# Expert activations turned by VectorE in 32x32 blocks, with gate and up strips taken in runs of 32 columns

## The chip, the cores and the metric

One core of one Trainium2 chip runs the kernel. The metric is the device time of one execution, in microseconds. One execution was also recorded by the hardware profiler, and all rows in this document come from such recordings.

## What is computed

One layer of a hybrid diffusion backbone over 640 tokens of 1024 values (128 context tokens, 512 latent tokens): a modulated norm, a token mixer (mLSTM heads and a Hyena long convolution), and then a mixture of experts. Everything is float32. The change touches the experts alone:

```python
def hier_moe(x, p):
    ...
    # coarse top-1 of 4 groups, then top-2 of 4 experts in it
    gates = jnp.sum(jax.nn.one_hot(expert_ids, N_EXPERTS, dtype=jnp.float32) * w_sel[..., None], axis=1)
    hg = jnp.einsum('td,edf->tef', xt, p['w_gate'])
    hu = jnp.einsum('td,edf->tef', xt, p['w_up'])
    act = jax.nn.silu(hg) * hu * gates[:, :, None].astype(x.dtype)
    return jnp.einsum('tef,efd->td', act, p['w_down']).reshape(bsz, seq_len, d)
```

There are 16 experts, each with a gate matrix and an up matrix of 1024 x 512 and a down matrix of 512 x 1024 (2 MiB each, 6 MiB per expert). Each token uses two experts.

## The kernel before

The program writes the instruction stream of each engine by hand and orders the engines by semaphores. The expert stage is the last large one. The tokens that chose an expert are packed into **groups** of 32 rows; each expert has at least two groups, and the profiled inputs give 48 groups in all. TensorE runs the groups in the order of the experts, in one hardware loop per expert (`pe.Fori`), and handles a group in three steps.

- **`gate_and_up(i, e)`** (matmul at L1919). The stationary operand is one 128 x 32 block of the group's input, `xg`, already turned. The array is split into four column strips of 32 (`LANES`, q = 0 to 3), and strip q computes hidden columns q*128 to q*128+127 of gate and of up at once, 256 columns in one moving operand. Over 8 blocks k of the contraction that makes 32 matmuls. The profile shows a float32 matmul as two records, so 64 records. The result stands in PSUM bank 2: partition 32q+r holds row r of the group, the first 128 columns are gate, the next 128 are up.
- **`down(i, e)`** (L1930), 16 matmuls or 32 records of 256 columns, again in four strips. The stationary operand is a 128 x 32 slice of `aT`, the turned activation, and the moving operand the down matrix. It runs one group behind: TensorE does `gate_and_up(i)`, `down(i - 1)`, `turn_act(i)`.
- **`turn_act(i)`** (L1938), one TensorE transpose of the whole 128 x 128 activation `uact` into PSUM bank 4.

The other engines work around this order. VectorE (loop at L1413 to L1424) turns the input rows of the next group in 32 x 32 blocks (`turn_rows`, L1400), multiplies silu(gate) by up into `uact` (L1420, signal `act_ready`), copies half of the down result out (`y_out`, L1407), and copies the turned activation from PSUM to SBUF as `aT` (L1424, signal `aT_d`). ScalarE computes silu (L868), copies the other half of the down result (L849) and issues the store of 128 KB to DRAM (L855). GpSimd issues an indirect load (L533) that gathers the rows of a later group, 32 rows of 4 KB.

The **weights** go through three sets of buffers. The SyncE queue issues the gate and up loads of expert e+3 once `gu_done` shows that the last gate-and-up of expert e has finished, and its down load once `down_done` shows the same of the last `down` (L436). At the start of an expert TensorE waits until its gate and up loads have landed (L1954), and before its first `down` for the down load. After the last group comes `y_out`, a gather of all expert outputs and the final norm, which use neither loads nor TensorE.

The waits that order a group on VectorE and TensorE:

```python
dve.wait_ge(S["at_t"], i)          # ahead of the multiply into uact
dve.wait_ge(S["at_t"], i + 1)      # ahead of the copy to aT
dve.wait_ge(S["down_done"], i)
pe.wait_ge(S["act_ready"], i)      # ahead of gate_and_up(i): bank 2 has been read
pe.wait_ge(S["aT_d"], i + 1)       # ahead of down(i)
```

Of the kernel before, what the change touches and what calls it, by code (L numbers as in the profile page):

```python
# [13 lines left out]
P = 128  # L14
D = 1024
KD = D // P
# [13 lines left out]
NG, NE, EPG = 4, 16, 4  # L30
FF = 512
LANE = 32
UNITS = 2 * H
ROWS = 36
LANE = 32
LANES = P // LANE
# [65 lines left out]
def emit(nc, a, stack):  # L102
# [7 lines left out]
    ps = stack.enter_context(nc.psum_tensor("banks", [P, 8, 512], F32))  # L110
# [67 lines left out]
    ident = small(128)  # L178
# [80 lines left out]
    set_at = [(0, F0 + 2 * SLOT, SLOT), (2 * SLOT, F0 + SLOT, F0), (W2 + 5120, W2 + 5120 + SLOT, W0)]  # L259
# [3 lines left out]
    xg = area(E0 + 512, KD, LANE)  # L263
    gact = area(E0 + 768, P)
    uact = area(E0 + 896, P)
    aT = area(E0 + 1024, P)
# [4 lines left out]
    def rt(*shape):  # L271
# [32 lines left out]
        e_ready w_ready s_done p_ready kw_ready inter_done inter_read intra_done num_ready upd_done st_ready  # L304
        h_ready hsq hss hrs yml_ready yt_done yt_read wo_done wo_sq wo_ss wo_rs x2_sq x2_rs h2_ready h2t_done h2t_read
        lg_done rt_v rt_exp pos_done idx_done tiles_ready route_ready
        idx_taken xg_ready gu_done silu_ready act_ready at_t aT_d down_done y_a y_d
        comb_s comb_v comb_rs fin_ready act_chain dve_chain pool_chain""".split()
    S = {n: sem(n) for n in names}
    ld_max = [sem(f"ld_max{i}") for i in range(2)]  # L310
# [42 lines left out]
    def start_at_one(eng, *signals):  # L353
        for name in signals:
            eng.sem_inc(S[name], 1)
# [535 lines left out]
    def _(dve):  # L891
# [32 lines left out]
        for o in range(ORD):  # L924
            for w in range(10):
                t, s, n = w // 2, w % 2, 20 * o + w
# [18 lines left out]
            for g in (1, 3, 5, 7):  # L945
# [12 lines left out]
                first, second = spec_h[:, o, part, blk + 1, :], ps[:, 1 + n % 4, :]  # L958
# [26 lines left out]
        for n in range(1, 10, 2):  # L985
# [6 lines left out]
            else:  # L992
                k = n - 2
# [4 lines left out]
        for n in range(12):  # L998
            part, blk = ((2, 0, 1)[n // 4], n % 4)
            dve.wait_ge(S["conv_a"], n + 1)  # L1000
            u = part1t[:, blk, :] if part == 1 else ubuf[:, n % 2, :]
# [190 lines left out]
        for i in range(NSTEP):  # L1192
            d, t = steps[i]
# [219 lines left out]
        with dve.Fori(0, pairs) as pair:  # L1413
            for n in range(2):
                i = 2 * pair + 1 + n
                dve.wait_ge(S["gu_done"], i + 1)
                turn_rows(1 - n, 16 * pair + 16 + 16 * n)
                dve.wait_ge(S["silu_ready"], i + 1)
                dve.wait_ge(S["at_t"], i)
                dve.tensor_tensor(uact, ps[:, 2, P:2 * P], gact, ALU.mult).then_inc(S["act_ready"], 1)  # L1420
                y_out(i - 1, n, 16 * pair + 16)
                dve.wait_ge(S["at_t"], i + 1)
                dve.wait_ge(S["down_done"], i)
                dve.tensor_copy(aT, ps[:, 4, 0:P]).then_inc(S["aT_d"], 1)  # L1424


        pairs = dve.value_load(tiles_i[0:1, 16:17], min_val=MINGROUPS // 2, max_val=GROUPS // 2)
# [10 lines left out]
        for t in range(NT):  # L1438
# [3 lines left out]
            s = st1[:, 60 + t:61 + t]  # L1442
# [4 lines left out]
    def _(pe):  # L1447
        M = pe.matmul
# [72 lines left out]
        for o in range(ORD):  # L1521
            for w in range(10):
                t, s, n = w // 2, w % 2, 20 * o + w
# [11 lines left out]
            for g in range(10):  # L1535
# [4 lines left out]
                if g >= 8:  # L1540
                    mm = M(ps[:, b, :], dft_c[:, 9 - g, :], ab[:, 9 - g, 0, :], start=True, stop=True)
                else:
                    f, odd = (g % 4) // 2 * P, (1 - g % 2) if part == 0 else g % 2
                    for i in range(2):
                        tb = 2 * odd + i
                        mm = M(ps[:, b, :], dft_l[:, tb, part, f:f + P], ab[:, part, 1 + tb, :], start=i == 0, stop=i == 1)  # L1546
                mm.then_inc(S["filt_done"], 1)
                if g == 0:
                    pe.wait_ge(S["lanes_read"], 2 * o + 2)
                    for i, rows in enumerate((P, 2 * LANE)):  # L1550
                        mm = M(ps[0:1, 5 + i, :], lane_pick[0:rows, :], lane_sums[i], start=True, stop=True)
# [4 lines left out]
                if g == 7:  # L1556
                    pe.wait_ge(S["norm_sqrt"], 2 * o + 2)
                    for i in range(2):
                        for blk in range(NB):
                            c = i * NB + blk  # L1560
                            mm = M(ps[:, 6, c:c + 1], norm_rows[i][:, blk * P:(blk + 1) * P], ones[0:1, 0:1],
                                   start=True, stop=True)
# [6 lines left out]
        for n in range(10):  # L1569
# [3 lines left out]
            for q in range(4):  # L1573
                t, k = (0, 4 * n + q) if n < 2 else (1 + q, n - 2)
                mm = pe.transpose(ps[:, b, q * P:(q + 1) * P], x_raw[:, t, k * P:(k + 1) * P], ident)
# [76 lines left out]
        for t in range(NT):  # L1652
            b = inverse_bank(t)
            if t < LT:
                for fb in range(2):
                    pe.wait_ge(S["mul_done"], fb + 1)
                    for part in range(2):
                        mm = M(ps[:, b, :], idft_l[:, fb, part, t * P:(t + 1) * P], spec_x[:, part, 2 * fb + t // 2, :],  # L1658
                               start=fb == 0 and part == 0, stop=fb == 1 and part == 1)
            else:  # L1660
                pe.wait_ge(S["mul_done"], 3)
                M(ps[:, b, :], dft_c[:, 2, :], spec_xc[:, 0, :], start=True, stop=False)
                mm = M(ps[:, b, :], dft_c[:, 3, :], spec_xc[:, 1, :], start=False, stop=True)
# [5 lines left out]
        for n in range(5):  # L1669
            b = inverse_bank(NT + n)  # L1670
            if n < NB:
                for r in range(2):
                    half = slice(r * LAT // 2, (r + 1) * LAT // 2)
                    for fb in range(2):
                        pe.wait_ge(S["mul_done"], 4 + fb)
                        for part in range(2):
                            mm = M(ps[:, b, half], spec_x[:, part, 2 * fb + r, n * P:(n + 1) * P],  # L1677
                                   idft_l[:, fb, part, half], start=fb == 0 and part == 0, stop=fb == 1 and part == 1)
            else:
                pe.wait_ge(S["mul_done"], 6)  # L1680
                for c in range(NB):
                    M(ps[:, b, c * P:(c + 1) * P], spec_xc[:, 0, c * P:(c + 1) * P], dft_c[:, 2, :], start=True, stop=False)
                    mm = M(ps[:, b, c * P:(c + 1) * P], spec_xc[:, 1, c * P:(c + 1) * P], dft_c[:, 3, :],
                           start=False, stop=True)
# [4 lines left out]
        for b, lo, hi in ((7, CTX, TOK), (0, 0, CTX)):  # L1689
            for step in range(KD // LANES):  # L1690
                for lane in range(LANES):
                    k = lane * (KD // LANES) + step
                    mm = M(ps[lane * LANE:(lane + 1) * LANE, b, 0:hi - lo], wgate[:, k, :], hT[:, k, lo:hi],
                           start=step == 0, stop=step == KD // LANES - 1)
# [3 lines left out]
        for t in range(NT):  # L1698
            if t >= 4:
                pe.wait_ge(S["qk_read"], 2 * NB + t - 3)  # L1700
            for h in range(H):
                mm = pe.transpose(ps[:, 1 + t % 4, h * P:(h + 1) * P], kT[:, h, t * P:(t + 1) * P], ident)
# [5 lines left out]
        for i in range(2):  # L1708
            M(ps[0:ROWS, 5 + i, :], gate_pick[:, i, :], gate_parts[:, CTX:TOK], start=True, stop=True)
            mm = M(ps[0:ROWS, 0, i * P:(i + 1) * P], gate_pick[:, i, :], gate_parts[:, 0:CTX], start=True, stop=True)  # L1710
# [26 lines left out]
        for n, (t0, t1) in enumerate(((0, 3), (3, 5))):  # L1737
            for t in range(t0, t1):
                for q in range(4):
                    c = ((t - t0) * 4 + q) * ROWS  # L1740
                    mm = pe.transpose(ps[:, 5 + n, c:c + ROWS], g_q[:, q, t * P:(t + 1) * P], ident[0:ROWS, 0:ROWS])
# [4 lines left out]
        for u in range(UNITS):  # L1746
            mm = M(ps[:, 7, u * NT:(u + 1) * NT], sel[:, u, :], dec, start=True, stop=True)
# [14 lines left out]
        for i in range(NSTEP):  # L1762
            d, t = steps[i]
# [124 lines left out]
        first = [1] + first_groups(1, 6)  # L1888

        def row_numbers(hot, lo, ready):  # L1890

            pe.wait_ge(S["rt_v"], ready)
            for n in range(2 * NT):
# [13 lines left out]
        first += first_groups(8, NE + 1)  # L1907

        gate_up = [mem[:, g:g + 2 * (u - g)].rearrange("p (s w) -> p s w", s=2)[:, :, 0:SLOT]
                   .rearrange("p s (k f) -> p s k f", k=KD) for g, u, d in set_at]  # L1910
        downs = [area(d, FF // P, D) for g, u, d in set_at]

        def gate_and_up(i, e):

            pe.wait_ge(S["xg_ready"], i + 2)
            pe.wait_ge(S["act_ready"], i)
            for k in range(KD):
                for q in range(LANES):
                    mm = M(ps[q * LANE:(q + 1) * LANE, 2, 0:2 * P].rearrange("p (g f) -> p g f", g=2), xg[:, k, :],  # L1919
                           gate_up[e % 3][:, :, k, q * P:(q + 1) * P], start=k == 0, stop=k == KD - 1)  # L1920
            mm.then_inc(S["gu_done"], 1)

        def down(i, e):
# [7 lines left out]
                           downs[e % 3][:, q, l * 256:(l + 1) * 256], start=q == 0, stop=q == FF // P - 1)  # L1931
            mm.then_inc(S["down_done"], 1)

        def turn_act(i):

            pe.wait_ge(S["act_ready"], i + 1)
            pe.wait_ge(S["aT_d"], i)
            pe.transpose(ps[:, 4, 0:P], uact, ident).then_inc(S["at_t"], 1)  # L1938

        start_at_one(pe, "gu_done", "down_done", "at_t")  # L1940
        for full in w_full[0][0:2]:
            pe.wait_ge(full, 16)
        gate_and_up(1, 0)
        turn_act(1)
        for e in range(NE):
            loads = 16 * (e // 3 + 1)
            with pe.Fori(first[e] + 1, first[e + 1]) as i:
                gate_and_up(i, e)
                pe.wait_ge(w_full[e % 3][2], loads)
                down(i - 1, e)  # L1950
                turn_act(i)
            if e + 1 < NE:
                for full in w_full[(e + 1) % 3][0:2]:
                    pe.wait_ge(full, 16 * ((e + 1) // 3 + 1))  # L1954
                gate_and_up(first[e + 1], e + 1)
            down(first[e + 1] - 1, e)
            if e + 1 < NE:
                turn_act(first[e + 1])


# [24 lines left out]
```

## Time and profile before

| | us |
|---|---|
| median of 3 runs | 918.48 |
| lowest, highest | 917.35, 919.62 |
| the profiled execution, its own time | 917.74 |
| its span, first to last instruction | 915.9 |
| TensorE busy | 827.9 (90% of the span) |
| VectorE, ScalarE, GpSimd busy | 409.7, 269.1, 107.0 |
| mean granted TensorE clock | 0.967 of full |
| data moved by DMA | 191.41 MB |

A row names the engine (PE is TensorE's matmuls, PEld its weight loads, DVE is VectorE, ACT is ScalarE, POOL is GpSimd, SPq the queue of SyncE), the line of the code, the operation, and the output and input tile. All SBUF tiles are parts of `arena`, and all PSUM tiles parts of `banks`, so that the line tells which tile it is. Matmuls overlap in the array: their starts show the pace, their durations do not add up.

### The profile page before, as it was taken

The page shows a single profiled execution, that of the slowest core. Times are in us where ns is not written, and L with a number is a line of the kernel's source. Part 1 is how long each engine was busy: PE and PEld are TensorE (multiplying, and loading weights), DVE is VectorE, ACT ScalarE, POOL GpSimd, SP SyncE. Part 2 cuts the span into 40 slices and gives each one's busy share as a digit, 9 for nine tenths or more (in the row PEclk, how much of TensorE's full clock was granted, in tenths as well). Part 3 has the DMA queues.
Part 4 walks back from the last instruction along what each step waited for, and adds up shares of the span by engine and source line. Part 5 has one row for each costly group of instructions (what it writes and reads, how often), then busy time and mean ns, then how long its engine had stood idle before and what let it go on. Part 6 is the DMA issues. An engine that isn't in the chain of part 4 may idle for free.

```text
span 915.9 us, 17241 instructions
## 1 busy us (share of the span) xinstructions
PE 827.9 (90%) x6857; PEld 449.2 (49%) x6857; DVE 409.7 (45%) x799; ACT 269.1 (29%) x541; POOL 107.0 (12%) x210
## 2 busy tenths in 40 slices
PE   5898999999999999997998999789999999999900
PEld 1242555555355457554664455455555555555500
DVE  5645721121492491555444774833333333333335
ACT  1676411210200100327232332123333333333332
POOL 4000000000001000001001000022222222222140
PEclk9999999999999999999999999799999999999965
DMA  8958303140705302033009203999999999995162
GB/s 258 414 229 321 127 1 115 69 184 1 275 1 171 109 1 92 24 116 115 1 1 340 119 24 132 418 352 412 417 422 416 418 420 415 419 421 195 41 243 113
DMA packets 40202, 191.41 MB, mean 209 GB/s; under 512 B 4416, under 2 KB 4712, under 8 KB 32529
## 3 DMA queue, kind: packets, MB, share of 16 engines
q1 hardware_dynamic: 28426, 152.50, 41.7%
q0 software_dynamic: 9168, 31.61, 10.0%
q10 hardware_dynamic: 2552, 6.50, 2.0%
q8 instruction: 43, 0.70, 0.3%
q14 instruction: 13, 0.11, 0.0%
HBM read 174.14 MB, written 16.44 MB: 208 GB/s over the span
## 4 chain that ended last, share of the span: by engine, by line
PE 81%; DVE 6%; DMA 5%; ACT 4%; issue 1%; SPq 1%; POOL 0%; DVEq 0%; ACTq 0%; POOLq 0%
PE banks L1919 19%; PE banks L1584 15%; PE banks L1930 9%; PE banks L1814 4%; PE banks L1585 4%; PE banks L1824 4%; PE banks L1546 3%; PE banks L1625 3%; PE banks L1720 3%; DMA arena<-in_w_ada 3%; PE banks L1729 2%; PE banks L1478 2%; ACT arena L755 2%; PE banks L1677 2%; PE banks L1658 1%
## 5 line engine op out<-in xcount | busy, mean ns | idle before, releaser
L1919 PE MATMUL banks<-arena 128*32 128x256 f32 x3072 | 175.7, 381 | 1.5 <-DVE arena L1400 1.5
L1584 PE MATMUL banks<-arena 128*128 128x512 f32 x320 | 164.2, 595 | 2.6 <-ACT arena L708 1.6
L1919 PEld LDWEIGHTS banks<-arena 128*32 128x32 f32 x3072 | 95.7, 110 | 64.9 <-issue 2.3
L1585 PEld LDWEIGHTS banks<-arena 128*128 128x128 f32 x320 | 60.8, 190 | 76.5 <-issue 76.5
L1400 DVE STREAM_TRANSPOSE arena<-arena 128x256 f32<-128x256 f32 x49 | 32.2, 656 | 137.3 <-PE banks L1919 134.4
L1930 PE MATMUL banks<-arena 128*32 128x256 f32 x1536 | 91.7, 379 | 1.0 <-DVE arena L1424 1.0
L1930 PEld LDWEIGHTS banks<-arena 128*32 128x32 f32 x1536 | 50.0, 110 | 33.8 <-DVE arena L1424 1.2
L1585 PE MATMUL banks<-arena 128*128 128x128 f32 x320 | 61.5, 274 | 0.0
L1407 DVE COPY arena<-banks 32x256 f32<-32x256 f32 x98 | 41.4, 422 | 40.6 <-PE banks L1930 39.9
L849 ACT ACTIVATE arena<-banks 32x256 f32<-32x256 f32 x98 | 36.6, 374 | 71.5 <-PE banks L1930 70.9
L1584 PEld LDWEIGHTS banks<-arena 128*128 128x128 f32 x320 | 48.5, 192 | 6.1 <-issue 4.9
L1007 DVE SCALAR_TENSOR_TENSOR arena<-banks,arena 128x504 f32<-128x504 f32 x12 | 8.9, 743 | 89.4 <-ACT arena L685 89.4
L533 POOL DMA_INDIRECT arena<-expert_input,arena x47 | 46.2, 984 | 12.5 <-issue 12.5
L868 ACT ACTIVATE arena<-banks 128x128 f32<-128x128 f32 x48 | 13.3, 277 | 99.0 <-PE banks L1919 99.0
L1729 PE MATMUL banks<-arena 128*128 128x512 f32 x80 | 37.7, 616 | 5.1 <-ACT arena L747 3.3
L865 ACT ACT_TABLE_LOAD x24 | 30.8, 1283 | 28.4 <-DVE arena L1407 22.1
L1814 PE MATMUL banks<-arena 128*128 128x512 f32 x80 | 36.8, 617 | 2.5 <-ACT arena L747 2.5
L1824 PE MATMUL banks<-arena 128*128 128x512 f32 x80 | 35.5, 597 | 1.7 <-DVE arena L1229 1.7
L684 ACT ACTIVATE arena<-banks,arena 128x512 f32<-128x512 f32 x12 | 8.2, 687 | 94.5 <-PE banks L1585 94.5
L1720 PE MATMUL banks<-arena 128*128 128x512 f32 x80 | 34.9, 595 | 0.0
L1546 PE MATMUL banks<-arena 128*128 128x512 f32 x64 | 28.8, 600 | 2.3 <-DVE arena L921 2.3
L530 POOL COPY arena<-arena 128x1 int32 x47 | 8.5, 181 | 182.0 <-DVE arena L1400 182.0
(380 smaller groups left out, 1025.2 us busy)
## 6 DMA issues: line engine op xcount, KB each, us to landing
arena<-in_w_gate SPq DMA_DIRECT2D x16, 2048.0 KB, 21.2
arena<-in_w_up SPq DMA_DIRECT2D x16, 2048.0 KB, 26.4
arena<-in_w_down SPq DMA_DIRECT2D x16, 2048.0 KB, 25.8
arena<-in_w_ada SPq DMA_DIRECT2D x12, 2048.0 KB, 13.7
arena<-in_w_in SPq DMA_DIRECT2D x7, 2048.0 KB, 7.9
expert_output<-arena ACTq DMA_DIRECT2D x49, 128.0 KB, 6.3
expert_output<-arena POOLq DMA_DIRECT2D x1, 4096.0 KB, 20.9
arena<-in_w_out SPq DMA_DIRECT2D x2, 2048.0 KB, 7.7
```

What stands on the lines that cost most here:

```text
L533: pool.indirect_dma_start(xr[n], None, h2_quarters, bass.IndirectOffsetOnAxis(ap=idx_now[n], axis=0))\
L849: ins = act.activation(ysb[n][:, l * 256:(l + 1) * 256], ps[l * LANE:(l + 1) * LANE, 5, 0:256], ACT.Copy)
L1407: ins = dve.tensor_copy(ysb[n][:, l * 256:(l + 1) * 256], ps[l * LANE:(l + 1) * LANE, 5, 0:256])
L1546: mm = M(ps[:, b, :], dft_l[:, tb, part, f:f + P], ab[:, part, 1 + tb, :], start=i == 0, stop=i == 1)
L1584: M(ps[:, b, :], lhs, hT[:, k, CTX:TOK], start=k == 0, stop=k == KD - 1)
L1585: mm = M(ps[:, b + 1, 0:CTX], lhs, hT[:, k, 0:CTX], start=k == 0, stop=k == KD - 1)
L1720: mm = M(ps[:, 1 + n % 4, :], hT[:, k, n * P:(n + 1) * P], w[:, k, :], start=k == 0, stop=k == KD - 1)
L1729: mm = M(ps[:, 1, :], hT[:, k, t * P:(t + 1) * P], w[:, k, :], start=k == 0, stop=k == KD - 1)
L1814: M(ps[:, 1 + 2 * (j % 2) + c, :], part1t[:, k, t * P:(t + 1) * P], w[:, NB + k, :], start=k == 0, stop=False)
L1824: mm = M(ps[:, 1 + 2 * (j % 2) + c, :], ymlT[:, k, t * P:(t + 1) * P], w[:, k, :], start=False, stop=k == NB - 1)
L1919: mm = M(ps[q * LANE:(q + 1) * LANE, 2, 0:2 * P].rearrange("p (g f) -> p g f", g=2), xg[:, k, :], gate_up[e % 3][:, :, k, q * P:(q + 1) * ...
L1930: mm = M(ps[l * LANE:(l + 1) * LANE, 5, 0:256], aT[:, q * LANE:(q + 1) * LANE], downs[e % 3][:, q, l * 256:(l + 1) * 256], start=q == 0, s ...
```

## The change

`turn_act` and its signal `at_t` go. VectorE now turns `uact` itself, from SBUF to SBUF, in place of its copy out of PSUM. Its transpose turns each 32 x 32 block where it stands, so block a of strip q, which holds four times 32 hidden columns, lands in partitions 32q to 32q+31 and columns 32a to 32a+31 of `aT`. For `aT[:, 32a:32a+32]` to be the 128 rows a*128 to a*128+127 that `down` wants, strip q must compute the columns a*128 + 32q + j (a = 0 to 3, j = 0 to 31). So the moving operand of `gate_and_up` takes four runs of 32 columns, 128 apart, in gate and again in up: 8 runs of 32 instead of 2 runs of 128. The down matrix and the loads stay as they are.

```diff
@@ VectorE, expert loop @@
                 dve.wait_ge(S["silu_ready"], i + 1)
-                dve.wait_ge(S["at_t"], i)
+                dve.wait_ge(S["aT_d"], i)
                 dve.tensor_tensor(uact, ps[:, 2, P:2 * P], gact, ALU.mult).then_inc(S["act_ready"], 1)
                 y_out(i - 1, n, 16 * pair + 16)
-                dve.wait_ge(S["at_t"], i + 1)
+                dve.wait_ge(S["act_ready"], i + 1)
                 dve.wait_ge(S["down_done"], i)
-                dve.tensor_copy(aT, ps[:, 4, 0:P]).then_inc(S["aT_d"], 1)
+                dve.transpose(aT, uact).then_inc(S["aT_d"], 1)
@@ TensorE @@
         gate_up = [mem[:, g:g + 2 * (u - g)].rearrange("p (s w) -> p s w", s=2)[:, :, 0:SLOT]
-                   .rearrange("p s (k f) -> p s k f", k=KD) for g, u, d in set_at]
+                   .rearrange("p s (k a q j) -> p s k q a j", k=KD, q=LANES, j=LANE) for g, u, d in set_at]
...
-                    mm = M(ps[q * LANE:(q + 1) * LANE, 2, 0:2 * P].rearrange("p (g f) -> p g f", g=2), xg[:, k, :],
-                           gate_up[e % 3][:, :, k, q * P:(q + 1) * P], start=k == 0, stop=k == KD - 1)
+                    mm = M(ps[q * LANE:(q + 1) * LANE, 2, 0:2 * P].rearrange("p (g a j) -> p g a j", g=2, j=LANE), xg[:, k, :],
+                           gate_up[e % 3][:, :, k, q, :, :], start=k == 0, stop=k == KD - 1)
...
-        def turn_act(i):
-
-            pe.wait_ge(S["act_ready"], i + 1)
-            pe.wait_ge(S["aT_d"], i)
-            pe.transpose(ps[:, 4, 0:P], uact, ident).then_inc(S["at_t"], 1)
...
         gate_and_up(1, 0)
-        turn_act(1)
         for e in range(NE):
             loads = 16 * (e // 3 + 1)
             with pe.Fori(first[e] + 1, first[e + 1]) as i:
                 gate_and_up(i, e)
                 pe.wait_ge(w_full[e % 3][2], loads)
                 down(i - 1, e)
-                turn_act(i)
...
             down(first[e + 1] - 1, e)
-            if e + 1 < NE:
-                turn_act(first[e + 1])
```

In TensorE's stream, the first expert's loop and the way into the second, before. L1947 is the loop, L1915 the wait for the next expert's gate and up loads:

```order
L1919 MATMUL banks<-arena 32x256 [waits act_ready,xg_ready]
L1919 MATMUL banks<-arena 32x256 x31
L1930 MATMUL banks<-arena 32x256 [waits y_a,y_d,aT_d,w_full02]
L1930 MATMUL banks<-arena 32x256 x15
L1936 REGISTER_ALU
L1938 MATMUL banks<-arena 128x128 [waits aT_d,act_ready]
L1947 REGISTER_ALU
L1947 COMPARE_AND_BRANCH
L1915 REGISTER_ALU [waits w_full11,w_full10]
L1919 MATMUL banks<-arena 32x256 [waits act_ready,xg_ready]
```

The same place with the change, where L1940 is the loop:

```order
L1919 MATMUL banks<-arena 32x256 [waits act_ready,xg_ready]
L1919 MATMUL banks<-arena 32x256 x31
L1930 MATMUL banks<-arena 32x256 [waits y_a,y_d,aT_d,w_full02]
L1930 MATMUL banks<-arena 32x256 x15
L1940 REGISTER_ALU
L1940 COMPARE_AND_BRANCH
L1915 REGISTER_ALU [waits w_full11,w_full10]
L1919 MATMUL banks<-arena 32x256 [waits act_ready,xg_ready]
```

The one matmul between `down` and the next `gate_and_up` is gone, with its two waits; all else keeps its place.

On VectorE, one group of the loop, as a piece of the difference:

```order
 L1400 STREAM_TRANSPOSE arena<-arena 128x256 [waits gather1]
 L1419 REGISTER_ALU [waits silu_ready]
-L1420 TENSOR_TENSOR arena<-banks,arena 128x128 [waits at_t]
+L1420 TENSOR_TENSOR arena<-banks,arena 128x128 [waits aT_d]
 L1407 COPY arena<-banks 32x256 [waits y_stored0,down_done]
 L1407 COPY arena<-banks 32x256
-L1424 COPY arena<-banks 128x128 [waits down_done,at_t]
+L1424 STREAM_TRANSPOSE arena<-arena 128x128 [waits down_done,act_ready]
```

The copy becomes a block transpose at the same place, and both waits on `at_t` become waits on VectorE's own earlier signals.

## Rows read from the trace of the kernel before

**Rows 1.** Page, part 4: the chain that ended last, shares of the span by line
```profile
PE banks L1919 19%; PE banks L1584 15%; PE banks L1930 9%; PE banks L1814 4%; PE banks L1585 4%; PE banks L1824 4%; PE banks L1546 3%; PE banks L1625 3%; PE banks L1720 3%; DMA arena<-in_w_ada 3%; PE banks L1729 2%; PE banks L1478 2%; ACT arena L755 2%; PE banks L1677 2%; PE banks L1658 1%
```
**Rows 2.** Timeline from 640 us: start, us, engine, line, op, out<-in, count, [idle before <-releaser]
```profile
640.24 3.66 PE L1919 MATMUL banks<-arena 128*32 128x256 f32 x64
...
643.72 1.91 PE L1930 MATMUL banks<-arena 128*32 128x256 f32 x32
...
644.06 0.66 DVE L1400 STREAM_TRANSPOSE arena<-arena 128x256 f32<-128x256 f32 x1 [2.76 <-PE banks L1919]
644.64 0.25 DVE L1420 TENSOR_TENSOR arena<-banks,arena 128x128 f32<-128x128 f32 x1
...
645.56 0.33 PE L1938 MATMUL banks<-arena 128*128 128x128 f32 x1
...
645.70 0.86 DVE L1407 COPY arena<-banks 32x256 f32<-32x256 f32 x2 [0.81 <-PE banks L1930]
645.82 3.18 PEld L1919 LDWEIGHTS banks<-arena 128*32 128x32 f32 x64
```
**Rows 3.** Timeline of PE, cut inside a group
```profile
642.86 1.05 PE L1919 MATMUL banks<-arena 128*32 128x256 f32 x16
...
644.80 0.83 PE L1930 MATMUL banks<-arena 128*32 128x256 f32 x12
```
**Rows 4.** The chain of waits in time: start, us, what
```profile
645.63 0.26 PE banks L1938
645.89 3.59 PE banks L1919 x64
649.48 1.73 PE banks L1930 x32
```
**Rows 5.** DMA, 20 us stretches: busy PE, PEld, DVE, ACT, POOL, clock, DMA share, GB/s
```profile
760.00:780.00 20.00, 20.00 (x352) 11.25 (x348) 7.15 (x18) 5.72 (x16) 4.93 (x12) 1.00 1.01 416
...
840.00:860.00 20.00, 20.00 (x352) 11.21 (x346) 7.18 (x19) 5.91 (x14) 5.43 (x12) 1.00 0.17 51
```
**Rows 6.** Up load issues of experts 8, 12 (SyncE), then each one's gate-and-up landing
```profile
683.39 0.44 SPq L436 DMA_DIRECT2D arena<-in_w_up  x1
DMA to landing us min/median/max: 22.7/25.3/27.9
...
750.33 0.43 SPq L436 DMA_DIRECT2D arena<-in_w_up  x1
DMA to landing us min/median/max: 23.4/25.9/28.5
```
**Rows 7.** Timeline of PE: starts of group 2, expert 8, expert 12, last group
```profile
606.77 3.66 PE L1919 MATMUL banks<-arena 128*32 128x256 f32 x64
...
718.34 1.93 PE L1919 MATMUL banks<-arena 128*32 128x256 f32 x32
...
785.28 3.66 PE L1919 MATMUL banks<-arena 128*32 128x256 f32 x64
...
863.39 3.66 PE L1919 MATMUL banks<-arena 128*32 128x256 f32 x64
```
**Rows 8.** Timeline of PE and DVE after the last gate-and-up
```profile
868.84 0.86 DVE L1407 COPY arena<-banks 32x256 f32<-32x256 f32 x2 [0.81 <-PE banks L1930]
869.73 0.29 DVE L1424 COPY arena<-banks 128x128 f32<-128x128 f32 x1
...
870.08 1.93 PE L1930 MATMUL banks<-arena 128*32 128x256 f32 x32 [1.04 <-DVE arena L1424]
```
**Rows 9.** Timeline of PE: small matmuls of 80 columns (L1875) and 64 (L1899)
```profile
585.72 0.45 PE L1875 MATMUL banks<-arena 128*128 128x80 f32 x2 [2.18 <-DVE arena L1330]
...
596.35 0.43 PE L1899 MATMUL banks<-arena 128*128 128x64 f32 x2 [0.43 <-DVE arena L1365]
```
**Rows 10.** PE after a long idle time, and the stretch around it (columns as rows 5)
```profile
432.12 5.26 PE L1729 MATMUL banks<-arena 128*128 128x512 f32 x8 [3.33 <-ACT arena L747]
...
430.00:436.00 6.00, 3.88 (x6) 1.77 (x7) 0.98 (x2) 1.95 (x3) 1.88 (x3) 0.72 0.39 88
```

More of the change, by code:

```diff
@@ L306, in emit @@
         lg_done rt_v rt_exp pos_done idx_done tiles_ready route_ready
-        idx_taken xg_ready gu_done silu_ready act_ready at_t aT_d down_done y_a y_d
+        idx_taken xg_ready gu_done silu_ready act_ready aT_d down_done y_a y_d
         comb_s comb_v comb_rs fin_ready act_chain dve_chain pool_chain""".split()
@@ L1932, in down @@
             mm.then_inc(S["down_done"], 1)
-        def turn_act(i):
-            pe.wait_ge(S["act_ready"], i + 1)
-            pe.wait_ge(S["aT_d"], i)
-            pe.transpose(ps[:, 4, 0:P], uact, ident).then_inc(S["at_t"], 1)
-        start_at_one(pe, "gu_done", "down_done", "at_t")
+        start_at_one(pe, "gu_done", "down_done")
         for full in w_full[0][0:2]:
```

## The prediction

> **What bounds the kernel now.** I read the page's chain first. The expert stage's two matmul lines, L1919 and L1930, make 28% of the span [rows 1], the largest share of any stage. The timeline then shows one group: gate-and-up from 640.24, down from 643.72, the turn at 645.56, the next gate-and-up at 645.82 [rows 2]. One group takes 5.58 us from gate-and-up to gate-and-up. TensorE has no idle time in it. VectorE and ScalarE wait for TensorE: VectorE sits idle 2.76 us before it turns the input rows [rows 2]. So in this stage each microsecond that TensorE saves counts, as long as nothing else is late.
>
> The DMA windows show what may be late. From 760 to 780 us the DMA share is 1.01, at 416 GB/s, and only at 840 to 860 is it down to 0.17 [rows 5]. The 16 DMA engines are full while experts are loaded. They are not on the chain before because the loads run ahead. How far ahead, the issue rows tell: the up load of expert 8 is issued at 683.39 and lands 27.9 us later, at 711.3, for a start of that expert at 718.34; that of expert 12 is issued at 750.33, lands at 778.8, and the expert starts at 785.28 [rows 6, 7]. The lead is 7.0 and 6.5 us. A faster TensorE can use that much and no more, as long as the transfers don't get faster too, and with full DMA engines an earlier issue doesn't make them so.
>
> **The change, part by part.**
>
> *The turn goes from TensorE.* What does it hold up? Within a phase four records, one per strip, start together. 16 records take 0.86 us (642.86 to 643.72) across the border from gate-and-up to down [rows 3, 2], so a four takes 0.216 us and that border costs nothing. The last 12 records of down start from 644.80 on [rows 3], so the last four starts at 645.23. The turn starts 0.33 us after it instead of 0.216, and the next gate-and-up 0.26 us after the turn [rows 2]. Without the turn a group is 24 fours x 0.216 = 5.18 us, against 5.58: **0.40 us per group**. The lower bound is the 0.26 us that the chain puts on the turn, beside 3.59 and 1.73 for the matmuls [rows 4]. I take 0.40, since the row of the unbroken border is the same kind of border that the change leaves behind. The Trainium skill (TensorEngine Tiling (Array Packing), Key Properties) says that changing the tiling mode drains TensorE; by this rule the change takes out two switches, into the full array and back, and the saving is more than the transpose itself, 0.40 and not 0.26. The late start of the turn agrees.
>
> *Strips with runs of 32.* The same 64 records, 256 columns each, now read in 8 runs instead of 2. No row shows this shape. The nearest: gate-and-up with 2 runs and down with 1 run keep the same 0.216 us. Farther off, two records of 80 columns whose input is 16 runs of 5 take 0.45 us, and two of 64 columns in one run take 0.43 us [rows 9]; the 16 extra columns alone explain the 0.02. I take zero, with a bound of 0.02 us per group for a gain or a loss by noise in these rows; a large price is a rival below. The output columns in PSUM are as contiguous as before.
>
> *The waits on TensorE.* The next gate-and-up still waits for `act_ready`, which the turn used to wait for. The multiply ends at 644.89, the last four of down starts at 645.23 [rows 2, 3]: 0.3 us to spare, and with the turn gone TensorE asks for it 0.6 us after it came (645.45). So the wait doesn't take the place of the turn. ScalarE's silu ends before the multiply and has the same cover.
>
> *VectorE: copy out, block transpose in.* The copy takes 0.29 us [rows 8]. The transpose of 128 x 256 takes 0.66 us [rows 2], so one of 128 x 128 costs between 0.33 (half of it) and 0.66; I take 0.37, nearer to the half, since its columns are halved. It follows the two copies of 0.86 us [rows 2]. `down` wants `aT` only after a whole gate-and-up of 3.5 us, and 0.86 + 0.37 lies well inside. It costs nothing there. The one place without cover is the last group, where the last down waits for it [rows 8]: +0.1 us. If the transpose took all the 0.66 us it would be +0.4.
>
> *The first group.* Group 2's gate-and-up starts at 606.77 [rows 7], right behind the turn of group 1, which no `down` covers. Without the turn it starts once the multiply is done. That saves between nothing and the turn's 0.26 us [rows 4]; I take 0.2, as only the multiply's wait stays.
>
> *Stores and gathers* keep their number (128 KB out and 128 KB in per group), but come closer together while the loads run.
>
> **The sum.** By TensorE alone: from group 2 (606.77) to the last group (863.39) there are 46 pitches [rows 7]; 0.2 + 46 x 0.40 - 0.1 = 18.5 us. But the loads set a floor. Expert 8 starts 20 pitches after group 2 ((718.34 - 606.77)/5.58): TensorE would be there 8.2 us earlier, and its lead is 7.0, so it waits about one us. Expert 12 starts 32 pitches after group 2; TensorE would be there 13.0 us earlier, and its load lands only 6.5 us before the old start. What moves that landing: -0.2, as the first refill is issued earlier; +0.6, as TensorE is one group ahead and so one more group's 0.26 MB passed at 416 GB/s [rows 5]. So it lands at 779.2, and TensorE starts about 0.4 us after a landing (an estimate between nothing and 0.67, the time from the multiply's end to the turn's start [rows 2], where the turn also waits for the array). That gives 779.6, a gain of 5.7 us. The experts from 13 on are safe: from 785.28 to 863.39 there are 14 pitches, 14 x 0.40 = 5.6 us more, and DMA falls to a share of 0.17 in this time [rows 5]. Then -0.1 at the last down. **5.7 + 5.6 - 0.1 = 11.2 us.** The tail is unchanged. 917.74 - 11.2 = 906.5 for the profiled execution; the median of the runs lay 0.7 above it, so **907.3**.
>
> With 0.26 us per group in place of 0.40, expert 12 still waits for its load, and the gain is 5.7 + 3.6 - 0.1 = 9.2 (909.3). That the landing moves by 2 us either way gives 905.3 to 909.3. Where an earlier expert's wait is long, nothing adds up: it only uses the same lead.
>
> **The rivals.**
>
> 1. *The loads keep up.* If earlier issues made earlier landings, the gain is 18.5 us and the time 900.0. For it: up loads take 28 us from issue to landing, so the queue is deep. Against it: a DMA share of 1.01 [rows 5], which leaves nothing to speed up. Chance 0.07.
>
> 2. *The waits for loads cost clock as well.* Before expert 12 TensorE would stand about 3 us or more, longer if the last down ends early. In this trace an idle time of 3.33 us stands before a stretch whose granted clock is 0.72 on average [rows 10], that is part of it at 1.2 GHz instead of 2.4. 0.28 x 6 us of that stretch is 1.7 us of lost work. After expert 12 that is not won back: 909.0. The Trainium skill (TensorE: Matmul & The Clock Gate, Why this matters for your kernels) warns against idle gaps between bursts of matmuls for this reason; by it the time would be this one. Against it: the stall I work out is a little shorter than the one in the row, since TensorE loses about 1 us at experts 8 to 10 already and arrives later. Chance 0.15.
>
> 3. *The runs of 32 read slower: slower than before.* Place: the 16 fours of gate-and-up in all 48 groups. If the start of a run cost time, there are 6 more per record. It decides from the point where it eats the 18.5 us of TensorE's gain: 18.5/48 = 0.39 us per group, 24 ns on each four of 216. For a result over 0.3% slower it takes 0.45 us per group, 28 ns per four, and the time is 921.3; at half the read rate it is +3.45 x 48 - 18.5 = +147 us, 1065. For it: no row has this shape. Against it: one or two runs make no difference, nor do 16 runs of 5 beyond 0.02 us [rows 9]. Chance 0.04.
>
> 4. *Something on the short loop is late*, such as the gathered rows of the next group, whose transfer shares the full DMA engines and now has two pitches of 5.18 instead of 5.58 to land. VectorE's 2.76 us idle before its turn of the input rows is put down to TensorE [rows 2], so the rows were there. If they came late by some 0.1 us in most groups up to expert 12, the load floor would hide it; it would cost only behind it, where DMA goes idle. Price up to 2 us: 909.3. Chance 0.07.
>
> **How the numbers follow.** The forecast, a gain bounded by the load of expert 12 or its neighbour, has 0.67. The range has to hold landings that move by 2 us, the smaller saving of 0.26, the clock rival, and part of the way to rival 1: 903.5 to 911.0. Outside are rival 1, rival 3 and the ends. About 0.3% (2.8 us) is what a measurement of this kernel can tell from no change. Everything but rival 3, and a small rest in which a partial read price meets the load floor, is faster by more than that: faster 0.93, same 0.03, slower 0.04.
>
> **What would show it.** Right: inside an expert the pitch is 5.18 us with no L1938; idle time of TensorE before L1919 at the starts of experts 8 to 12 that ends on a landing of `in_w_up`; the DMA share stays 1.0 to about 837 us; the block transpose at L1424 takes 0.33 to 0.45 us; the last gate-and-up starts some 11 us before 863.39. Wrong: a four of gate-and-up longer than 0.216 us (rival 3), no idle time at expert starts (rival 1), a granted clock under 1.0 behind a wait (rival 2), VectorE's turn of the rows waiting for a gather (rival 4).

## The result and the profile after

The changed kernel takes **911.76 us** (median of 4 runs, 909.31 to 913.53), the kernel before 918.85 (4 runs): ratio 0.9916, 95% interval 0.9891 to 0.9940, 7 to 8 us faster. Run again beside three of the experiments it took 911.11 against 920.48, ratio 0.9903 (0.9885 to 0.9922). The forecast of 907.3 had the direction right; the time lies 0.8 us above its range. The profiled execution took 909.31, the fastest of the four, so it is set against 917.74.

One group of the loop, from the changed kernel's timeline (columns as in rows 2; L1424 is now the block transpose):

```profile
641.45 1.94 PE L1930 MATMUL banks<-arena 128*32 128x256 f32 x32
...
641.81 0.66 DVE L1400 STREAM_TRANSPOSE arena<-arena 128x256 f32<-128x256 f32 x1 [2.47 <-PE banks L1919]
...
642.50 0.29 DVE L1420 TENSOR_TENSOR arena<-banks,arena 128x128 f32<-128x128 f32 x1
...
643.18 3.66 PE L1919 MATMUL banks<-arena 128*32 128x256 f32 x64
...
644.23 0.29 DVE L1424 STREAM_TRANSPOSE arena<-arena 128x128 f32<-128x128 f32 x1
...
646.63 1.94 PE L1930 MATMUL banks<-arena 128*32 128x256 f32 x32
```

From one down to the next it is 646.63 - 641.45 = 5.18 us, where rows 2 had 5.58 for a group. The next gate-and-up starts 1.73 us after down, with nothing between. It takes 3.45 us from its start to the next down with its 8 runs, where rows 2 have 3.48 with 2 runs.

TensorE's starts that answer to rows 7 and 8, from the same timeline:

```profile
602.14 3.66 PE L1919 MATMUL banks<-arena 128*32 128x256 f32 x64
606.92 3.66 PE L1919 MATMUL banks<-arena 128*32 128x256 f32 x64 [1.12 <-DVE arena L1420]
...
713.01 3.66 PE L1919 MATMUL banks<-arena 128*32 128x256 f32 x64 [1.92 <-DMA arena<-in_w_up]
...
729.37 3.66 PE L1919 MATMUL banks<-arena 128*32 128x256 f32 x64 [0.61 <-DMA arena<-in_w_up]
...
746.55 3.66 PE L1919 MATMUL banks<-arena 128*32 128x256 f32 x64 [1.43 <-DMA arena<-in_w_up]
...
781.74 5.15 PE L1919 MATMUL banks<-arena 128*32 128x256 f32 x64 [3.90 <-DMA arena<-in_w_up]
786.70 1.92 PE L1930 MATMUL banks<-arena 128*32 128x256 f32 x32
...
862.33 1.93 PE L1930 MATMUL banks<-arena 128*32 128x256 f32 x32 [1.19 <-DVE arena L1424]
```

TensorE waits for the up load at experts 8, 9, 10 and 12, 7.9 us in all. The prediction had about 1 us for experts 8 to 10; they took 4.0, but each of these waits only uses up the same lead. The page's chain now has `DMA arena<-in_w_up` at 8%. The first gate-and-up of expert 12 takes 4.96 us instead of 3.45. The windows say why (columns as in rows 5):

```profile
612.00:775.00 163.00, 158.88 (x2936) 114.81 (x2931) 61.40 (x153) 54.33 (x123) 41.72 (x92) 1.00 1.01 417
...
780.00:790.00 10.00, 8.27 (x128) 4.99 (x132) 2.01 (x5) 1.02 (x3) 1.36 (x3) 0.83 1.03 429
```

The granted clock was full up to there, with the DMA engines full; behind the idle time of 3.90 us it is 0.83 over 10 us, as much as 3.4 us at 1.2 GHz instead of 2.4. That costs 4.96 - 3.45 = 1.5 us.

The start of the stage moves by some microseconds from execution to execution (601.78 before, 602.14 and 599.96 in two profiles of the changed kernel). So I compare the **stage length**, from TensorE's first gate-and-up to its last down: 870.08 - 601.78 = 268.30 before, 862.33 - 602.14 = 260.19 after, 260.54 in the second profile. The stage gives 8.1 of the profiled 8.4 us. The two pairs of medians, 7.1 and 9.4 us apart, lie on both sides of it.

### The profile page after: what moved, and what is told of

It is laid out like the page before. It is cut to its first block, busy times and chain, and to the rows that moved or that the text cites. A ratio compares the mean times of both kernels' runs of the same rounds, so it can differ in the third digit from the quotient of the medians.

```text
span 907.5 us, 17049 instructions
## 1 busy us (share of the span) xinstructions
PE 813.7 (90%) x6809; PEld 470.7 (52%) x6809; DVE 411.5 (45%) x799; ACT 269.0 (30%) x541; POOL 107.6 (12%) x210
## 4 chain that ended last, share of the span: by engine, by line
PE 74%; DMA 12%; DVE 6%; ACT 4%; issue 1%; SPq 1%; POOL 0%; DVEq 0%; ACTq 0%
PE banks L1584 15%; PE banks L1919 14%; DMA arena<-in_w_up 8%; PE banks L1930 6%; PE banks L1585 4%; PE banks L1824 4%; PE banks L1814 4%; PE banks L1546 3%; PE banks L1625 3%; PE banks L1720 3%; DMA arena<-in_w_ada 3%; PE banks L1729 2%; PE banks L1478 2%; ACT arena L755 2%; PE banks L1677 2%; PE banks L1658 2%
## 5 line engine op out<-in xcount | busy, mean ns | idle before, releaser
L1919 PE MATMUL banks<-arena 128*32 128x256 f32 x3072 | 177.1, 382 | 9.1 <-DMA arena<-in_w_up 7.9
L1919 PEld LDWEIGHTS banks<-arena 128*32 128x32 f32 x3072 | 115.4, 111 | 62.7 <-issue 12.5
L1930 PEld LDWEIGHTS banks<-arena 128*32 128x32 f32 x1536 | 57.6, 110 | 26.6 <-DVE arena L1424 1.7
```

Source lines behind the costliest of these rows:

```text
L1930: mm = M(ps[l * LANE:(l + 1) * LANE, 5, 0:256], aT[:, q * LANE:(q + 1) * LANE], downs[e % 3][:, q, l * 256:(l + 1) * 256], start=q == 0, s ...
```

## The experiments

All are timed against the kernel before on the same chip; the rows come from several chips, so compare ratios and stages rather than medians. Stage length as above; the start of expert 12 is counted from the start of the stage.

| kernel | median us | ratio to before, 95% | stage us | expert 12 at |
|---|---|---|---|---|
| before | 918.85 | | 268.30 | 183.50 |
| changed | 911.76 | 0.9916 (0.9891-0.9940) | 260.19 | 179.60 |
| changed, again | 911.11 | 0.9903 (0.9885-0.9922) | 260.54 | 179.75 |
| runs of 32 alone | 920.33 | 1.0004 (0.9987-1.0022) | 268.34 | |
| VectorE's turn alone | 911.77 | 0.9912 (0.9880-0.9943) | 260.49 | 179.71 |
| before, light loads | 920.08 | 0.9999 (0.9981-1.0017) | 268.29 | |
| changed, light loads | 900.71 | 0.9793 (0.9765-0.9821) | 249.64 | |
| light, runs of 128 | 900.61 | 0.9795 (0.9773-0.9817) | 249.63 | |
| light, two turns | 900.00 | 0.9778 (0.9761-0.9794) | 249.94 | |
| two down loads smaller | 909.17 | 0.9875 (0.9854-0.9897) | 257.67 | 176.89 |
| filler at expert 12 | 909.33 | 0.9884 (0.9864-0.9903) | 258.69 | 179.60 |
| halves | 910.84 | 0.9904 (0.9881-0.9928) | 259.72 | |
| halves, early refill | 909.41 | 0.9881 (0.9861-0.9901) | 257.07 | |
| halves, early, filler | 908.79 | 0.9871 (0.9852-0.9889) | 257.63 | |
| no gathers | one run | | 249.64 | |
| more SyncE code | one run | | 263.26 | 182.48 |

**1. Each half of the change alone.** Runs of 32 with TensorE's turn kept:

```diff
# the kernel before, plus
+                   .rearrange("p s (k a q j) -> p s k q a j", k=KD, q=LANES, j=LANE) for g, u, d in set_at]
+                           gate_up[e % 3][:, :, k, q, :, :], start=k == 0, stop=k == KD - 1)
```

> The kernel before with only the runs of 32 in gate-and-up; TensorE keeps its turn, so down multiplies activations with rows of the down matrix that belong to other columns. Theory (the gain is capped by the weight loads, and the runs of 32 are free): same as before within 0.3%, pitch of a group 5.58 us, a four of gate-and-up 0.216 us. Rival (runs of 32 cost reading time, and this took part of the gain): slower by 1 to 4 us, pitch above 5.6 us.

The stage is 268.34 us, as before. A group of this kernel in the timeline:

```profile
644.30 3.66 PE L1919 MATMUL banks<-arena 128*32 128x256 f32 x64
647.78 1.91 PE L1930 MATMUL banks<-arena 128*32 128x256 f32 x32
649.62 0.33 PE L1938 MATMUL banks<-arena 128*128 128x128 f32 x1
649.88 3.66 PE L1919 MATMUL banks<-arena 128*32 128x256 f32 x64
```

5.58 us, and 3.48 from gate-and-up to down as in rows 2. The other half, VectorE's turn with the strips' old columns (the `gate_up` lines of the kernel before in the changed kernel):

> The changed kernel with the strips' old columns (2 runs of 128): only the turn moves to VectorE, and down multiplies activations with rows of the down matrix that belong to other columns. Theory: as the changed kernel, 909 to 913.5 us, pitch 5.18 us, waits for up loads at expert 8 to 12. Rival (runs of 32 cost): faster than the changed kernel by 1 to 4 us.

911.77 us, stage 260.49: the whole gain is in the turn, for in the stage the two full kernels lie 7.8 to 8.1 us apart and this one 7.8. The runs of 32 are only needed so that `down` meets the right rows, and they cost nothing.

**2. The load floor taken away.** In both kernels experts 3 to 15 load a quarter of the down matrix, so that the loads run well ahead of TensorE. (The rest of each down buffer holds an older expert's rows; TensorE's work is the same.)

```diff
                 sp.wait_ge(S[done], used)
+                if done == "down_done":
+                    dst, src = dst[:, 0:1, :], src[:, 0:1, :]
                 sp.dma_start(dst, src).then_inc(full, 16)
```

> The kernel before, where experts 3 to 15 load only the first quarter of their down matrix (1.5 MiB less of 6 per expert; the rest of the buffer holds an older expert's rows). Theory: TensorE never waited for loads before, so nothing changes: within 0.3% of before. Rival (full DMA engines also slow the pace of TensorE or the late tail): 1 to 5 us faster.

> The changed kernel with the same quarter of down loads from expert 3 on. Theory (load floor): no waits on up loads, no fall of the clock at expert 12, the whole 46 pitches x 0.40 us come out: 18 us under the light kernel before, near 900 us, and runs that scatter less. Rival (the floor is something else, such as gathers or a wait in the loop): stays at 905 to 912 us.

The kernel before doesn't change (268.29). The changed one falls to 900.71 us, and its stage to 249.64: 18.7 us shorter than before, where TensorE's side of the sum said 18.5. No wait for a load is left among TensorE's waits over the stage:

```profile
PE banks L1921 <- DVE arena L1402: 1.4, 1, 1.4
PE banks L1932 <- DVE arena L1426: 1.2, 1, 1.2
PE banks L1901 <- DVE arena L1367: 1.1, 1, 1.1
PE banks L1921 <- DVE arena L1422: 1.1, 1, 1.1
```

and its window shows DMA engines that are not full, with the clock at 1.00:

```profile
612.00:775.00 163.00, 163.00 (x3028) 118.81 (x3024) 63.54 (x159) 56.40 (x127) 43.65 (x96) 1.00 0.92 369
```

So of the 18.7 us that the missing turn is worth, 10.5 to 10.9 are lost again to the weight loads and to the clock that falls behind a wait for them.

**3. The same floor, moved by a known amount.** The down loads of experts 3 and 4 alone bring three of four quarters:

```diff
                 sp.wait_ge(S[done], used)
+                if done == "down_done" and e in (3, 4):
+                    dst, src = dst[:, 0:3, :], src[:, 0:3, :]
                 sp.dma_start(dst, src).then_inc(full, 16)
```

> The changed kernel where the down loads of experts 3 and 4 bring only three quarters (0.5 MB less each, 2.5 us less for the DMA engines at 416 GB/s; the last quarter holds an older expert's rows). Theory (until expert 12 the DMA engines set the pace): start of expert 12 comes 2.5 us earlier after the start of the stage, its wait stays near 3.8 us, time 2.5 us under the changed kernel. Rival (the waits come from single late loads): the wait at expert 12 and the time stay as they were within 1 us.

Expert 12 starts 176.89 us into the stage instead of 179.60 and 179.75: 2.7 to 2.9 us earlier. The stage is 2.5 to 2.9 us shorter. (The medians, 909.17 against 911.11 and 911.76, agree, but their intervals overlap.) The wait is still there:

```profile
779.89 5.35 PE L1921 MATMUL banks<-arena 128*32 128x256 f32 x64 [3.71 <-DMA arena<-in_w_up]
```

So up to expert 12 the DMA traffic sets the pace: 2.5 us of it taken away came out as 2.5 to 2.9 us. The rival, single late loads, falls.

**4. What hides on VectorE, and the runs without a floor.** On the light changed kernel:

```diff
+                dve.transpose(fold, uact)
                 dve.transpose(aT, uact).then_inc(S["aT_d"], 1)
```

> The light changed kernel (down loads quartered from expert 3 on), where VectorE turns the activation twice in every group, the first time into an unused tile. Theory (VectorE's turn is hidden, but for the last group): 0.3 us over the light changed kernel, 900 to 902 us. Rival (VectorE is near the bound once TensorE is faster): 0.29 us in each group, 14 us more.

> The light changed kernel with the strips' old columns (2 runs of 128), where no load floor can hide a price of the runs of 32. Theory: as the light changed kernel within 1 us, the same 3.45 us from the first record of gate-and-up to the first of down. Rival (runs of 32 cost): faster by over 1 us.

A second turn in all 48 groups adds 0.30 us to the stage. Of it 0.19 is at the last down, the only place without cover, whose wait grows from 1.19 to 1.38 us; 0.1 comes once, at an expert's start 41 us into the stage, and I don't know from what. In all other groups it is hidden. With runs of 128 the stage is 249.63, with runs of 32 249.64: no price of the runs can be seen, 0.01 us over 48 groups.

**5. The clock at expert 12.** The filler:

```diff
+            if e + 1 in FILL:              # FILL = {12: 4}
+                stay_busy(FILL[e + 1])
             if e + 1 < NE:
                 for full in w_full[(e + 1) % 3][0:2]:
```

> The changed kernel with four idle matmuls of 128x512 (3.4 us, result unused) that TensorE runs ahead of its wait for the loads of expert 12, where it stood 3.9 us. Theory (the wait also costs clock: 3.4 us at 1.2 GHz, 1.5 us of work): granted clock stays at its high level at expert 12, 0.5 to 1.5 us faster than the changed kernel, less than the full 1.5 if the landing comes before the filler ends. Rival (the clock's fall costs nothing that counts): same as the changed kernel, or slower by the filler's overhang.

```profile
777.37 3.70 PE L1872 MATMUL banks<-arena 128*128 128x512 f32 x8
781.35 3.66 PE L1920 MATMUL banks<-arena 128*32 128x256 f32 x64 [0.28 <-issue]
784.80 1.94 PE L1931 MATMUL banks<-arena 128*32 128x256 f32 x32
```

Expert 12 starts at the same 179.60, but its gate-and-up takes 3.45 us again, and the stage is 1.5 to 1.9 us shorter than the changed kernel's, where 0.5 to 1.5 was expected. The medians, 909.33 and 911.11, say the same, though their intervals overlap. The clock's fall costs 1.5 us or a little more, near the 1.7 worked out from rows 10.

**6. Taking time off the floor.** Gate and up loads in two halves each; then the first half refilled from the middle of the old expert's last gate-and-up (`gu_half`); then with a filler of three between the halves:

```diff
+            for h in range(2):
+                for i, src in enumerate(srcs[0:2]):
+                    k = slice(KD // 2 * h, KD // 2 * (h + 1))
+                    yield area(set_at[e % 3][i], KD, FF)[:, k, :], src[:, k, :], w_full[e % 3][h]
...
             for k in range(KD):
+                if k == KD // 2 and second is not None:
+                    pe.wait_ge(w_full[e % 3][1], second)
...
+                if k == KD // 2 - 1:
+                    mm.then_inc(S["gu_half"], 1)
```

> The changed kernel with each expert's gate and up loads cut in two along the contraction: first blocks 0 to 3 of both, then 4 to 7; the first gate-and-up of an expert starts on the first halves and waits for the second in its middle. Theory (waits on the landing of up loads cap the gain): expert 12 finishes its first gate-and-up up to 1.7 us earlier after the landing, and the long idle time is cut in two shorter ones, so the clock may stay high: 1.5 to 3 us faster than the changed kernel, 907.5 to 910. Rival (total DMA time alone sets the pace, whatever the order in an expert, or the smaller loads land later): same as the changed kernel within 1 us, or slower.

> As the kernel with halves, and the first halves of a set are refilled once TensorE is half through the old expert's last gate-and-up, 1.7 us earlier. In the trace the DMA engines stand idle for about 3 us between the first nine loads (607.5) and the first refill (610.5). Theory: all later landings come 1.7 us earlier, so 1 to 2 us faster than the halves alone, 906 to 908.5. Rival (the landings follow from something else than the start of the refills): same as the halves alone.

> Halves, early refill, and three idle matmuls of 128x512 (2.6 us) between the two halves of the first gate-and-up of expert 12. Theory (waits and the clock's fall add up): no fall of the clock at expert 12, half a gate-and-up less behind the landing, 1 to 2 us faster than the halves with early refill (909.4) or than the filler alone (909.3): 907.5 to 908.5. Rival (what is saved before expert 12 only makes its wait longer): 909 to 910, as these two.

The halves alone miss their 907.5 to 910: 910.84 us, not to be told from the changed kernel (the stage is 0.5 to 0.8 us shorter). TensorE ran the first half ahead of the landing, but then stood as long in its middle, and the clock fell all the same:

```profile
777.21 1.91 PE L1924 MATMUL banks<-arena 128*32 128x256 f32 x32
783.02 2.57 PE L1924 MATMUL banks<-arena 128*32 128x256 f32 x32 [3.90 <-DMA arena<-in_w_up]
```

With the early refill the stage is 257.07 us, 2.6 less than with the halves alone, where 1 to 2 was expected. The refill itself gave 1.0 of it: the second half of expert 12 starts 179.69 us into the stage instead of 180.65, not 1.7 earlier. The rest comes from the clock, which did not fall in this execution, although the wait was 3.79 us:

```profile
783.14 1.94 PE L1924 MATMUL banks<-arena 128*32 128x256 f32 x32 [3.79 <-DMA arena<-in_w_up]
```

So its median of 909.41 (906 to 908.5 expected) is no proof of what the refill is worth. All three together give **908.79 us**, the fastest by its median of those that do the whole computation, 1.3% under the kernel before; its interval still touches that of the changed kernel. I expected 907.5 to 908.5. The filler brought the stage nothing there (257.63): the clock had not fallen without it in that profile, and the load landed 0.6 us later.

**7. Why the landing was late.** The up load of expert 12 lands at 781.39 in the changed kernel, issued at 745.16 with 36.2 us to its landing:

```profile
745.16 0.56 SPq L436 DMA_DIRECT2D arena<-in_w_up  x1
...
DMA to landing us min/median/max: 31.4/33.8/36.2
```

That is 179.3 us into the stage, against 177.1 before. The trace has 16 steps of the load's semaphore as it lands, with the time of each. There are 16 DMA engines, and I read each step as one engine's piece of the load. Before and after, the first piece of expert 12's up load came 173.7 and 173.9 us into the stage, and the last 3.4 and 5.4 us behind the first. It is not one piece alone that moved: the first is 0.1 us later than before, the mean of the 16 is 0.8 later, the last but one 1.1 and the last 2.2. The repeat of the changed kernel has the same picture (5.6 us between first and last). Nor is so wide a spread new: the kernel before has 5.7 us at expert 13, where nobody waits for the load.

Two kernels ask what makes the last piece late. Without the gathers of the loop, so that experts compute on old rows:

```diff
-            pool.indirect_dma_start(xr[n], None, h2_quarters, bass.IndirectOffsetOnAxis(ap=idx_now[n], axis=0))\
-                .then_inc(gather[n], 16)
+            pool.dma_start(xr[n][0:1, :], h2_quarters[0:1, :]).then_inc(gather[n], 16)
```

> The changed kernel where the 47 gathers of 128 KB inside the loop become loads of one row of 1 KB, so experts compute on old rows. In the changed kernel the first of the 16 pieces of expert 12's up load lands 5.4 us before the last; in the kernel before it was 3.4 us. Theory A (the gathers load the 16 DMA engines unevenly): the spread falls under 2 us. Theory B (it is code fetches or the weight loads themselves): the spread stays at 3 us or more. Both: 33 x 0.13 MB less before expert 12, so its landing comes about 10 us earlier, no waits for loads, the stage as short as in the light kernel (249.6 us from its first matmul to the last down).

The spread stays at 4.5 us, so the gathers are not what mainly makes it. Their bytes, though, were part of the floor: expert 12's load lands 11.8 us earlier, there are no waits for loads, and the stage is 249.64 us. With more code on SyncE, after each expert's loads:

```diff
                 sp.dma_start(dst, src).then_inc(full, 16)
+            for _ in range(192):
+                sp.wait_ge(S["ld_setup"], 112)
```

> The changed kernel where SyncE passes 192 waits that are already met after each expert's loads, so that its code fetches (16 KB pieces of the instruction queues, 1.0 to 1.1 us each on a DMA engine) grow by about 13 between experts 3 and 15. Theory B1 (code fetches hold up single DMA engines, and so the last piece of a load): more than 24 fetches in the stage, and the spread of expert 12's up load grows from 5.4 by 1 us or more. Rival (fetches spread evenly): the spread stays at 5.4 within 1 us.

The fetches show in part 3 of its page, in the second of the two instruction queues. The changed kernel has 13 packets there:

```profile
q8 instruction: 42, 0.69, 0.3%
q14 instruction: 23, 0.19, 0.1%
```

There are 10 more, not the 13 expected, and they are smaller than I had written, 8 KB and 0.3 us each. The spread grew from 5.4 to 8.5 us at expert 12. The first piece did not come later (173.7 us into the stage) and neither did the last but one (177.6 against 178.1), so it is not that SyncE issued the loads too late: one piece alone fell back. The eight more packets up to there take 2.5 us in all, so even if all of them held up the same engine, about 0.5 of the 3.1 us stays unexplained. The wait at expert 12 is 4.29 us, the stage 3.1 us longer:

```profile
785.39 5.35 PE L1921 MATMUL banks<-arena 128*32 128x256 f32 x64 [4.29 <-DMA arena<-in_w_up]
```

So more code on SyncE delayed the last piece of expert 12's load, in one profile. Whether fetches also make up the 2.0 us by which the changed kernel's spread exceeds that before is not shown. From 612 to 775 us the other instruction queue has 16 packets of 16 KB, about 1.1 us each, and the kernel before has 15 there: one more packet is half of the 2.0 us at most. The trace doesn't say which engine takes a packet, and no kernel with less code was run. The cause stays open.

## Why the prediction was right and wrong

- **The turn.** Right: 5.18 us per group, so 0.40 saved and not 0.26. The turn cost 0.14 us beyond its own 0.26, and without the floor the whole chain is 18.7 us shorter against 18.5 worked out. That this part is a drain of the array fits, but no run tells it from another cost of the switch.
- **Runs of 32.** Right at zero; rival 3 is out (experiments 1 and 4).
- **VectorE.** Right that it hides (experiment 4); the block transpose takes 0.29 us, the same as the copy, so my 0.37 was too high. The last down waits 1.19 us instead of 1.04.
- **The load floor.** Right mechanism and places: waits at experts 8, 9, 10 and 12, a DMA share of 1.01, and the floor moves with the bytes (experiments 2 and 3). Rival 1, loads that keep up, did not happen.
- **The failed step** is the term "What moves that landing", with its -0.2 and +0.6 us. It had expert 12's landing 0.4 us later than before, and so the expert's start at 779.6, 177.8 us into the stage. The landing came 2.2 us later, and the expert started at 179.60, 1.8 us after the forecast; the 0.4 us from landing to start was right. I took all pieces of a load to move together. On average they came 0.8 us later, but TensorE waits for the last, and that one came 2.2 later. What pushed it back further than the rest stays open (experiment 7).
- **The second part of the miss** is rival 2, given 0.15: the clock fell behind the wait, for 1.5 us where I said 1.7. The argument against it, that the stall would be a little shorter than 3.33 us, failed with the landing: it was 3.90. The Trainium skill (TensorE: Matmul & The Clock Gate, Why this matters for your kernels) warns of this, and six profiles here agree: each with a wait of 3.7 to 4.3 us at expert 12 lost clock behind it. One does not: the early refill, with 3.79 us, kept it. The waits of up to 1.98 us at experts 8 to 10 never cost clock. The filler of experiment 5 shows that the wait is the cause, for with TensorE kept busy the clock stayed up.
- **The sum** for the stage: 268.30 - 11.2 = 257.1 expected, 260.19 measured. 1.8 us is the landing and 1.3 lies behind expert 12's start, where the clock's 1.5 is set off by small differences.
- **The step to the median.** The profiled execution came 2.8 us above the 906.5 worked out for it, and the median lies another 2.4 above that execution, where I had added 0.7 from three runs of the kernel before. So 1.7 of the 4.5 us between 907.3 and 911.76 is scatter that the sum does not explain, and whether the median fell inside or outside the range of 903.5 to 911.0 is partly luck. Four executions from 909.31 to 913.53 don't tell why; in the repeat the six lay between 907.90 and 913.64, with a median of 911.11.
- **Rival 4** did not decide. VectorE waited three times, 7.3 us in all, for gathered rows, and TensorE stood for none of them inside the loop.
- **The range.** Counted from the stage's start, the landing stayed within its 2 us either way. But a late landing makes the stall long, and a long stall makes the clock fall, so the two errors come together with one sign. I had counted them as separate.

## What to carry to other kernels

When a saving is larger than the lead that the loads have at some point, the gain up to that point is about the lead: read, per expert, landing against first use, before counting instructions. Where the DMA engines are full, leave room for the last of a load's pieces to slip further than the mean rate says (here 2.2 us against 0.4 forecast), and count a long wait and its cost in clock together. Taking the one 128-wide operation out of this stream of 32-wide strips was worth more than its own time, 0.40 us against 0.26.

## What the runs showed that I had not expected

- The pieces of a load drift apart while the DMA engines are full: in the changed kernel the 16 pieces of a 2 MB up load land within 2.4 us at expert 3, 3.8 at expert 10 and 5.4 at expert 12. In the light kernel with runs of 128, with a DMA share of 0.92, it is 2.5 us at expert 12. More code on SyncE, eight packets of 0.3 us up to there, went with 3.1 us more.
- The stage's length repeats to 0.05 us where loads don't bind (268.30, 268.34, 268.29; 249.64, 249.63, 249.64), while the whole time scatters by 4 us: the three profiled executions with 268.3 took 917.74, 921.5 and 922.03 us. So that scatter comes from outside this stage.
- VectorE's multiply at L1420 takes 0.29 us in the changed kernel and 0.25 before [rows 2], also with VectorE's turn alone. It is hidden and I didn't look for its cause.
- A wait of 3.79 us once left the granted clock at its full level, where waits of 3.71 and 3.75 us in other kernels lowered it.
